# Rotary partners of queries and keys: permutation matmuls on TensorE, and transfers within SBUF

## The reference

```python
h = rms_norm(x, attn_norm_g[i])
proj = h @ w_in[i]
q, k, v, u, vv = jnp.split(proj, split_at, axis=-1)
q = rms_norm(q.reshape(b, s, N_HEADS, HEAD_DIM), q_norm_g[i])      # 8 heads of 64
k = rms_norm(k.reshape(b, s, N_KV_HEADS, HEAD_DIM), k_norm_g[i])   # 2 heads of 64
q = axial_rope(q, tables)
k = axial_rope(k, tables)
attn_o = gqa_attention(q, k, v)
sg_o = spatial_gating(jax.nn.gelu(u), jax.nn.gelu(vv), ...)

def rotate(x, cos, sin):
    x1, x2 = x[..., :n], x[..., n:]
    return jnp.concatenate([x1 * c - x2 * s, x2 * c + x1 * s], axis=-1)
```

## Time and profile before

| | us |
|---|---|
| median of three runs | 2470.47 |
| lowest, highest | 2470.42, 2472.21 |
| the profiled execution | 2471.41 |
| its span in the trace | 2469.6 |

### The profile page before, as it was taken

How to read it: one execution, slowest core, us unless ns; L and a number is a source line. 1 busy time by engine, 2 the same in 40 slices (tenths; PEclk the granted TensorE clock), 3 DMA queues, 4 the chain that set the end, 5 groups by cost and what they waited for, 6 DMA issues and landing times.

```text
span 2469.6 us, 33292 instructions
## 1 busy us (share of the span) xinstructions
PE 2395.6 (97%) x11691; PEld 1950.5 (79%) x11691; DVE 1470.7 (60%) x2142; ACT 1078.4 (44%) x1458; POOL 164.3 (7%) x159
## 2 busy tenths in 40 slices
PE   8998999999899989999999899999999989999998
PEld 6766888888788878888887677888888767888887
DVE  7886554532676636554326766887533686687732
ACT  5345433332456645334224553554423463454421
POOL 2010100000100011000002021000011012000000
PEclk9999999999999999999999999999999999999999
DMA  7331233333222222333333202333334202233331
GB/s 173 69 88 51 82 103 95 91 94 100 73 76 69 76 68 85 94 100 91 94 103 87 60 1 77 111 102 94 93 94 125 62 18 59 86 102 93 98 94 64
DMA packets 400951, 209.67 MB, mean 85 GB/s; under 512 B 18131, under 2 KB 397655, under 8 KB 400871
## 3 DMA queue, kind: packets, MB, share of 16 engines
q1 hardware_dynamic: 397111, 199.65, 28.2%
q0 software_dynamic: 3424, 8.91, 1.4%
q10 hardware_dynamic: 336, 0.05, 0.0%
HBM read 204.38 MB, written 4.19 MB: 84 GB/s over the span
## 4 chain that ended last, share of the span: by engine, by line
PE 87%; DVE 8%; ACT 2%; issue 1%; DVEq 1%; DMA 0%; ACTq 0%; SPq 0%
PE bank L677 70%; PE bank L723 4%; PE bank L727 2%; DVE tmp L1937 1%; DVE w_lo L1905 1%; PE bank L1288 1%; DVEq L1934 1%; PE bank L1264 1%; DVE small L2685 1%; PE bank L1239 1%; PE bank L1160 1%; PE bank L1202 0%; PE bank L753 0%; ACT w_hi L1362 0%; PE bank L1118 0%
## 5 line engine op out<-in xcount | busy, mean ns | idle before, releaser
L1905 DVE TENSOR_TENSOR w_lo<-w_raw,w_hi 128x1024 fp32r<-128x1024 f32 x380 | 472.2, 1243 | 544.9 <-ACT w_hi L1362 539.8
L677 PE MATMUL bank<-h_hi,w_hi 128*128 128x512 f32 x1840 | 727.1, 395 | 7.0 <-DVEq L1934 5.9
L677 PE MATMUL bank<-h_lo,w_hi 128*128 128x512 f32 x1840 | 717.4, 390 | 0.0
L677 PE MATMUL bank<-h_hi,w_lo 128*128 128x512 f32 x1840 | 716.8, 390 | 0.0
L1362 ACT ACTIVATE w_hi<-w_raw 128x1024 fp32r<-128x1024 f32 x380 | 401.6, 1058 | 667.7 <-PE bank L677 650.4
L677 PEld LDWEIGHTS bank<-h_hi,w_hi 128*128 128x128 f32 x1840 | 346.5, 188 | 82.4 <-DVEq L1934 6.0
L677 PEld LDWEIGHTS bank<-h_hi,w_lo 128*128 128x128 f32 x1840 | 346.3, 188 | 72.9 <-issue 2.9
L677 PEld LDWEIGHTS bank<-h_lo,w_hi 128*128 128x128 f32 x1840 | 345.8, 188 | 72.9
L677 PE MATMUL bank<-hid_hi,w_hi 128*128 128x512 f32 x704 | 273.9, 389 | 0.0
L677 PE MATMUL bank<-hid_hi,w_lo 128*128 128x512 f32 x704 | 273.9, 389 | 0.0
L677 PE MATMUL bank<-hid_lo,w_hi 128*128 128x512 f32 x704 | 273.9, 389 | 0.0
(11 more groups left out here) (466 smaller groups left out, 2866.2 us busy)
## 6 DMA issues: line engine op xcount, KB each, us to landing
w_raw<-in_ffn_w SPq DMA_DIRECT2D x120, 512.0 KB, 3.8
w_raw<-in_w_up SPq DMA_DIRECT2D x88, 512.0 KB, 3.8
w_raw<-in_c_w_in SPq DMA_DIRECT2D x32, 512.0 KB, 4.1
w_raw<-in_w_down SPq DMA_DIRECT2D x32, 512.0 KB, 3.7
w_raw<-in_w_in SPq DMA_DIRECT2D x28, 512.0 KB, 3.9
w_raw<-in_w_o SPq DMA_DIRECT2D x16, 512.0 KB, 3.8
w_raw<-in_ab_w_in SPq DMA_DIRECT2D x12, 512.0 KB, 6.1
w_raw<-in_ffn_w SPq DMA_DIRECT2D x16, 384.0 KB, 3.3
```

Of the source, the lines that this page charges most:

```text
L677: mm = nc.tensor.matmul(out[:], w[:, s, k], v[:, kt], start=(kt == 0 and w is w_hi and v is hi), stop=(kt == sum(slabs) - 1 and v is lo))
L1905: nc.vector.tensor_tensor(w_lo[:, s], w_raw[:, s], w_hi[:, s].bitcast(F32), ALU.subtract).then_inc(lo_done, 1)
```

## The change

The ten partner matmuls (five in each of the two layers) go. In their place POOL issues, for each place, eight DMAs from `qa` to `tmp`, each of 16 partitions and 2 KB a partition, source and destination 16 partitions apart: 40 a layer, 80 in all. DVE waits for a place's eight DMAs instead of for the matmul, and multiplies the partner with `sin` in place. Two semaphores alternate between places, and POOL waits before places 2, 3 and 4 until the place two before has landed; place 4 also waits until DVE is through with place 0 (its buffer), by `q_roped`.

```diff
-PARTNERS = ((4, 5), (0, 6), (1, 7), (2, 5), (3, 6))
+PARTNERS = (4, 0, 1, 2, 3)
...
+        qk_moved = [sem(f"qk_moved{v}") for v in range(2)]
...
+                pool.wait_ge(qk_in, i + 1)
+                for place_, j in enumerate(PARTNERS):
+                    moved = qk_moved[place_ % 2]
+                    if place_ >= 2:
+                        pool.wait_ge(moved, n.now(moved))
+                    if place_ == 4:
+                        pool.wait_ge(q_roped, 4 * i + 1)
+                    for r in range(8):
+                        to, at_ = (P // 8) * r, (P // 8) * (r ^ 1)
+                        pool.dma_start(tmp[to:to + P // 8, place_ % 4], qa[at_:at_ + P // 8, j]).then_inc(moved, 16)
+                    n(moved, 16 * 8)
                 add_parts(gated_ready, [ua[:, j] for j in range(4)], ua_sum, ua_summed)
...
-                def partners(tiles):
-
-                    for j, b in tiles:
-                        nc.tensor.matmul(take(b)[:], turn, qa[:, j], start=True, stop=True).then_inc(qk_partner, 1)
-
-                pe.wait_ge(qk_in, n(qk_in))
-                partners(PARTNERS[:3])
...
-                partners(PARTNERS[3:])
...
-                for place_, (j, b) in enumerate(PARTNERS):
+                for place_, j in enumerate(PARTNERS):
                     a_ = tmp[:, place_ % 4]
-                    dve.wait_ge(qk_partner, n(qk_partner))
-                    tt(a_, bank[b][:], sin, ALU.mult)
+                    moved = qk_moved[place_ % 2]
+                    dve.wait_ge(moved, n(moved, 16 * 8))
+                    tt(a_, a_, sin, ALU.mult)
                     tt(qa[:, j], qa[:, j], cos, ALU.mult)
                     settle()
-                    flag(bank_free[b])
```

More of the change, by code:

```diff
@@ L373, in program @@
         s5 = {k: sem(f"s5_{k}") for k in ("pe_to_vector", "pe_to_scalar", "vector_to_pe", "scalar_to_pe")}
-        qk_squared, qk_in, qk_summed, qk_rooted, qk_inverted, qk_spread, qk_partner, k_turned, q_turned = (
-            sem(f"qk_{k}") for k in ("squared", "in", "summed", "rooted", "inverted", "spread", "partner", "k", "q"))
+        qk_squared, qk_in, qk_summed, qk_rooted, qk_inverted, qk_spread, k_turned, q_turned = (
+            sem(f"qk_{k}") for k in ("squared", "in", "summed", "rooted", "inverted", "spread", "k", "q"))
+        qk_moved = [sem(f"qk_moved{v}") for v in range(2)]
         k_swapped, v_in, v_turned, v_copied = (sem(k) for k in ("k_swapped", "v_in", "v_turned", "v_copied"))
```

## The result

| | before | changed |
|---|---|---|
| median of the runs, us | 2471.34 (4 runs, 2470.42 to 2473.18) | 2457.65 (4 runs, 2457.02 to 2459.71) |
| profiled execution, us | 2471.41 | 2459.71 |
| its span, us | 2469.6 | 2457.8 |

The ratio is 0.9945, 95% interval 0.9928 to 0.9962: 13.7 us less at the medians, 11.8 in the spans of the two profiled executions. In a second comparison the changed kernel took 2459.03 against 2471.33 (0.9946, 0.9932 to 0.9959). Faster, as forecast (2459.9). A fourth run of the kernel before lifted its median from the 2470.47 that the forecast started from to 2471.34.

The account below looks back on a forecast made before the run. PE, 97% busy, was taken to bound the kernel, with DVE and ACT next. 2 x (6.3 - 1.0) = 10.6 us off 2471.41 gives 2460.8, less 0.94 to the median: 2459.9 us; range 2457 to 2472, the forecast's own 2457 to 2464.

Parts of the forecast that it names:

- The first group: First three partner matmuls, ahead of tile 11: removal gains 2.9 us on PE, not their 5.29, tile 11 starting at 1.2 GHz.
- The second group and the wait for bank 6: Last two partner matmuls and PE's wait before the gating transposes: worth 1.9 and about 2.2 us a layer on PE.
- VectorE and ScalarE let 6.3 us through, not 7.0: Up to the end of L1193, DVE and ACT limit the gain to 6.3 us a layer, where PE alone would give 7.0.
- A place's pitch stays 2.03 us: On DVE, a place's three instructions stay and take 2.03 us as before; the operand now in SBUF changes nothing.
- Place 2 is late by 1.0 us: Place 2's transfers land 0.1 to 1.9 us after DVE needs them; 1.0 us a layer was taken off the gain.
- Nothing outside the two stretches: What arrives earlier at 1391.43, the end of tile 8, is earlier at the end; the first layer's gain counted twice.
- Middling transfers: Rival, chance 0.15: POOL's DMAs take 0.62 us each and 4.7 to landing; gain 2.5 us a layer, 2465.5 us.
- slow issue: Rival, chance 0.14: each DMA occupies POOL for 0.90 us, every place waits, 6.0 us a layer lost, 2482.5 us.
- The tipping point: POOL's issue time at which gain turns to loss: 0.75 us a DMA with 3.0 us to landing, 0.70 with 4.7.
- Serial transfers: Rival, chance 0.02: a place's eight DMAs land one after another, 24 us a place, some 80 us a layer late, near 2640.
- Absorbed: Rival, chance 0.07: a queue between L1193 and 1391.43 takes back PE's saved time; no change, 2470.5 us.

Follow-up runs that it names:

- the second trace: The changed kernel profiled again without a further edit; measured 2459.03 us against 2471.33 for the kernel before.
- the twelve pieces: Changed kernel with every second of a place's eight DMAs cut in two, same bytes; 2471.20 us against 2471.09 for the kernel before, ratio 1.0000.
- sixteen pieces: Changed kernel with each place's bytes in sixteen DMAs of eight partitions instead of eight of sixteen; 2498.54 us, ratio 1.0106.

## Why the prediction was right, and where it was off

- **The first group is worth 2.9 us, since tile 11 moves into the slow stretch.** Right. Tile 11 through at 1351.7 forecast, L1175 at 1351.73. Measured from the sums' start, tile 11 is through 2.72 us earlier. The clock rose between 1348.6 and 1349.0, where I had it at 1349.0. Done alone: 2.67 in the first layer. Its length in the trace, 5.29, would have been too much by a factor of nearly two. It does not hold for both layers: in the second the clock was back at 1.00 after half the time, and TensorE gained 4.3 us there.
- **The second group and the wait for bank 6, 4.1 us on TensorE.** Right: 4.3 alone, of which 3.86 come out.
- **VectorE and ScalarE let 6.3 us through, not 7.0.** Right: 6.41 and 6.26. TensorE reached L1197 at 1371.43 (forecast 1371.8), bank 7 was free at 1372.8 (1373.7), L1197 ended at 1373.94 (1374.2). The clearest proof came by itself: in the second layer the slow stretch was shorter and tile 11 was through 1.6 us earlier (11.61 us behind the sums' start for 13.24) than in the first. TensorE then stood 1.61 us before L1197, and the stretch was no shorter. ScalarE's reordered copies took 0.58 and 0.75 off.
- **A place's pitch stays 2.03 us.** Off: it is 1.93 (1346.67, 1348.60, 1350.53). With the first group by DMA alone it is 1.93 too, with that group by matmul 2.04. The flag that frees the bank went with the bank, and I had counted the three instructions alone; whether it is the flag or the operand in PSUM was not separated. It made VectorE 0.5 us faster over five places.
- **Place 2 is late by 1.0 us, and that comes off the gain.** This term was too large, and why it came to so little is in part luck. An issue took 0.484 us and not 0.53, and the landing 1.7 to 2.1 without a weight load beside it and up to 4.0 with one (4.2 in the second trace), where I had taken 3.0 to 4.7 throughout. In the first layer place 2's last transfer was issued before the load began and landed in 1.9 us; the load fell on place 3, which had slack, and no place waited. In the second layer the load fell on place 2, as forecast, its last transfer took 4.0 us, and place 2 waited 0.99 (1.25 in the second trace), but VectorE had started 0.9 us earlier there (place 0 is 7.26 us behind the sums' start, 8.18 in the first layer), because the slow stretch began later within the sums. That earlier start made up for the wait. Gain forecast 5.3 a layer, measured 6.3. The Trainium skill's fixed cost of about 2.0 us per DMA (DMA: Bandwidth & Descriptors, "Anatomy of one DMA — SWDGE (gpsimd) path") agrees with the landing where no load runs beside it, 1.7 to 2.1, and is short by up to 2.0 beside one. The 12.6 us which that sentence gave is what the two stretches gained, 12.7, though in the second layer place 2 was not in time.
- **Nothing outside the two stretches.** Off by the 1.8 us between the layers. The two misses are of opposite sign and about equal (2.0 and 1.8), and 0.8 us fell off behind the second stretch; so the span came out 11.8 us shorter where 10.6 were forecast. That the number came so near is luck as far as these cancel. The medians lie 13.7 apart, and 2457.65 is 0.65 above the lower end of the forecast's own range, 2457; without the 1.8 us it would have lain below it.
- **The rivals.** Middling transfers (0.62 an issue, 4.7 to landing) and slow issue (0.90): neither, 0.484. The tipping point of 6.0 us a place was measured by the twelve pieces. Beyond it the sum was too small: sixteen pieces cost 11.8 and 13.5 us a layer against before, where the prediction's working with 0.492 us an issue and 3.0 to landing gives 9.7; 1.1 of the rest is the low clock at the `vv` transposes. Serial transfers: no; eight issued 0.484 us apart were whole 1.8 to 4.0 us behind the last issue and 5.1 to 7.4 behind the first, and not 16 to 24. By its own terms that rival's sum was also too small: 24 us a place puts place 4 94 us past 1361.5, not some 80. The Trainium skill says that two transfers serialise (SBUF — State Buffer, "Can I just issue two DMAs to hit both halves?") of the rate of two transfers to two halves of SBUF, 6% more than one alone. The prediction stretched it to their landings, and for those it does not hold here; what it says of the rate no run here shows. Absorbed: no.

## What to carry to other kernels

Before a piece is taken off the bounding engine, ask at which clock it stood: what comes next can move into the slow stretch, and a group that takes 5.3 us in the trace may be worth 2.7. When the bounding engine becomes faster by several microseconds, work out the path of the engines that it hid; here it set the end at once, by 0.6 us. For small DMAs from GpSimd count the issues (0.48 us each) against the consumer's pace, and find the point where it tips: eight a place were free in one layer and cost a wait of 1 us in the other, twelve ate the whole gain, sixteen made the kernel 27 us slower than before.

## What was unexpected of the hardware

- Transfers within SBUF of 32 KB, forty in a row beside 512 KB weight loads and a VectorE that was 86% busy, slowed no VectorE instruction: a place that does not wait takes 1.93 us with them and without, and from place 0 to place 4 the first layer takes 14.37 us with them and 14.48 without.
- Halving a transfer's bytes (32 to 16 KB) left the issue where it was: 0.484 us for eight pieces a place, 0.499 for the mixed twelve, 0.492 for sixteen.
- The granted clock is not a function of the program alone. The same kernel at the same place showed 0.56 and 1.00, worth 4.0 us in one stretch. The clock fell behind idle times of TensorE (2.36 us in one layer and not in the other) and also while the engine was busy without a gap (sums of two columns, in a group or spread in a tile). An edit that shortens a kernel by 1 us can therefore be clear in its stretch and invisible in the total, and stretches should be compared before totals are.
